# Seven-product pairs from the second pair on in FFN 2 to 4, all weight sums on GpSimd, rows scaled per pair, bank runs in down pairs

## What is computed

```python
for l in range(DEPTH):                       # DEPTH = 2
    x = x + 0.5 * swiglu(rmsnorm(x, norm_w[l, 0]), ffn_w_gate[l, 0], ffn_w_up[l, 0], ffn_w_down[l, 0])
    h = rmsnorm(x, norm_w[l, 1])
    ...                                      # y = mLSTM mixer (l = 0) or gated linear attention (l = 1)
    x = x + y
    x = x + 0.5 * swiglu(rmsnorm(x, norm_w[l, 2]), ffn_w_gate[l, 1], ffn_w_up[l, 1], ffn_w_down[l, 1])
out = rmsnorm(x, final_norm_w)

def rmsnorm(x, w):
    xf = x.astype(jnp.float32)
    y = xf * lax.rsqrt(jnp.mean(xf * xf, axis=-1, keepdims=True) + EPS)
    return (y * w.astype(jnp.float32)).astype(x.dtype)

def swiglu(x, w_gate, w_up, w_down):
    return (jax.nn.silu(x @ w_gate) * (x @ w_up)) @ w_down
```

## Time and profile before

| | |
|---|---|
| median of 3 runs | 2209.91 us (2209.09 to 2210.4) |
| the profiled execution | 2210.02 us, its span 2208.2 us |
| granted TensorE clock, mean | 0.994 |
| PE busy | 2171.4 us, 98% of the span, 16360 matmuls |
| DVE, ACT, POOL busy | 1436.5, 937.9, 236.1 us |
| chain that ended last | PE 93%, DVE 4%, ACT 2% |

### The profile page before, as it was taken

How to read it: one execution, slowest core, us unless ns; L and a number is a source line. 1 busy time by engine, 2 the same in 40 slices (tenths; PEclk the granted TensorE clock), 3 DMA queues, 4 the chain that set the end, 5 groups by cost and what they waited for, 6 DMA issues and landing times.

```text
span 2208.2 us, 40072 instructions
## 1 busy us (share of the span) xinstructions
PE 2171.4 (98%) x16360; PEld 2148.8 (97%) x16360; DVE 1436.5 (65%) x2031; ACT 937.9 (42%) x1371; POOL 236.1 (11%) x186
## 2 busy tenths in 40 slices
PE   7999999999999999999999999999999999999997
PEld 7999999999999999999999999999999899999997
DVE  6797546585555787636678863754766457876365
ACT  5435435454433444525444452544322434445252
POOL 0112010001100002101000210100011101021110
PEclk9999999999999999999999999999999999999998
DMA  5223312223332222222322222232122222223222
GB/s 186 70 87 102 106 67 86 95 83 136 101 118 81 81 93 86 91 82 87 108 72 87 86 95 96 88 94 88 47 98 84 97 77 87 87 88 104 85 77 72
DMA packets 72574, 201.55 MB, mean 91 GB/s; under 512 B 7268, under 2 KB 26980, under 8 KB 72448
## 3 DMA queue, kind: packets, MB, share of 16 engines
q1 hardware_dynamic: 72448, 199.80, 27.7%
HBM read 187.82 MB, written 11.95 MB: 90 GB/s over the span
## 4 chain that ended last, share of the span: by engine, by line
PE 93%; DVE 4%; ACT 2%; issue 1%; DMA 0%; POOL 0%; SPq 0%; DVEq 0%; POOLq 0%
PE ps L525 49%; PE ps L583 33%; PE ps L800 4%; PE ps L655 1%; PE ps L831 1%; PE ps L820 1%; DVE w_lo L1821 1%; PE ps L834 0%; PE ps L850 0%; PE ps L664 0%; DMA x<-in_x 0%; PE ps L678 0%; PE ps L843 0%; PE ps L844 0%; DVE x L2641 0%
## 5 line engine op out<-in xcount | busy, mean ns | idle before, releaser
L525 PE MATMUL ps<-h_lo,w_hi 128*128 128x288 f32 x1616 | 351.4, 297 | 4.1 <-DVE h_hi L2306 4.1
L525 PE MATMUL ps<-h_hi,w_hi 128*128 128x288 f32 x1616 | 351.1, 296 | 0.7 <-DVE w_lo L1821 0.7
L583 PE MATMUL ps<-th_hi,w_hi 128*128 128x288 f32 x1088 | 320.9, 295 | 0.7 <-DVE ps L1916 0.7
L583 PE MATMUL ps<-th_hi,w_lo 128*128 128x288 f32 x1088 | 321.2, 295 | 0.0
L583 PE MATMUL ps<-th_lo,w_hi 128*128 128x288 f32 x1088 | 320.4, 294 | 0.0
L525 PE MATMUL ps<-h_hi,w_lo 128*128 128x288 f32 x1360 | 295.1, 296 | 0.0
L1821 DVE TENSOR_TENSOR w_lo<-raw,w_hi 128x1024 fp32r<-128x1024 f32 x196 | 232.0, 1220 | 65.7 <-ACT w_hi L1232 64.0
L525 PE MATMUL ps<-xn_hi,w_hi 128*128 128x288 f32 x1152 | 257.4, 301 | 11.7 <-DVE w_lo L1821 9.5
L525 PEld LDWEIGHTS ps<-h_lo,w_hi 128*128 128x128 f32 x1616 | 262.6, 189 | 4.8 <-DVE h_hi L2306 4.5
L525 PEld LDWEIGHTS ps<-h_hi,w_hi 128*128 128x128 f32 x1616 | 262.6, 189 | 1.0 <-DVE w_lo L1821 0.9
L525 PE MATMUL ps<-xn_lo,w_hi 128*128 128x288 f32 x1152 | 252.1, 296 | 0.0
(11 more groups left out here) (292 smaller groups left out, 4226.8 us busy)
## 6 DMA issues: line engine op xcount, KB each, us to landing
raw<-in_w_gu SPq DMA_DIRECT2D x176, 512.0 KB, 3.9
raw<-in_w_down SPq DMA_DIRECT2D x64, 512.0 KB, 4.3
raw<-in_w_mix SPq DMA_DIRECT2D x64, 512.0 KB, 4.2
raw<-in_w_down SPq DMA_DIRECT2D x32, 384.0 KB, 3.6
state_s<-in_state_c SPq DMA_DIRECT2D x4, 1024.0 KB, 7.8
out_c_s<-state_s SPq DMA_DIRECT2D x4, 1024.0 KB, 4.6
state_s<-in_state_g SPq DMA_DIRECT2D x4, 1024.0 KB, 6.6
out_s_s<-state_s SPq DMA_DIRECT2D x4, 1024.0 KB, 4.7
```

The lines of the kernel that those rows point to most:

```text
L525: ins = nc.tensor.matmul(o, a, b[:, c] if c is not None else b, start=first and j == 0, stop=last and j == 2)
L583: ins = nc.tensor.matmul(ps[:, bank, FIRST], left, b_, start=first and k == 0 and j == 0, stop=k == KT_X // 2 - 1 and j == 2, skip_group_c ...
```

## The change

In FFN 2 to 4 the plain pairs of group 0 fall from 5 to 1 (`PLAIN`); FFN 1 keeps 5. For this the tile sums of these FFNs are made in the phase ahead, on the last D or OUT phase: `x_ready` adds `early_even`, `u_sums`, `u_high` and `u_low` to the work per down pair. All four weight sums are GpSimd's (`pair_sums`), and in group 0 they wait until the squares have been added (`ssq_done`). `weights_low` now waits for the fourth. x is no longer scaled (`t_sums`, `t_high` are gone); every seven-product pair is scaled by `rows_scale`. The sums over the partitions are fed into PE's second block of pair 0 (`feed_sums`), ACT reads them with Ln and makes `rstd` with Exp, and PE waits after pair 0 for the Ln (`var_ready`), in FFN 1 too. In down pairs of `half` 0 the second block is done in bank runs. Signs of sums change.

```diff
-SEVEN_FROM = 5
+PLAIN = (5, 1, 1, 1)
...
                         if first_norm and half == 0:
-                            ins = token_sums(ph["norm"])
-                        ins.then_inc(pe_done, 1)
-                if consumer:
+                            pe.wait_ge(var_ready, ph["norm"] + 1)
+                if consumer and ph["skip"] > 1:
                     iteration(0, first_norm=True, bank_wait=ph["base"] > 0, by_bank=(1,))
                     iteration(1)
                     iteration(2, seven=(1,))
                     iteration(3, seven=(0, 1))
+                elif consumer:
+                    iteration(0, first_norm=True, seven=(1,))
+                    with pe.Fori(1, ph["pairs"] // 2) as i:
+                        iteration(i, seven=(0, 1))
                 else:
                     with pe.Fori(0, ph["pairs"] // 2) as i:
-                        iteration(i, seven=(0, 1) if ph["kind"] == "G" else ())
+                        iteration(i, by_bank=(0,) if ph["kind"] == "D" else (),
+                                  seven=(0, 1) if ph["kind"] == "G" else ())
...
+            def feed_sums(norm):
...
+                pe.wait_ge(ssq_done, 4 * (norm + 1))
...
+                for c in range(2):
+                    ins = nc.tensor.matmul(ps[:, 5 + 2 * c, FIRST], ones, half_of(T(5), c), start=True, stop=True)
+                ins.then_inc(feed_done, 1)
...
+            def feed_log(ph):
+
+                act.wait_ge(feed_done, ph["ffn"] + 1)
+                nc.scalar.activation(cut2(T(7)), ps[:, 5:8:2, FIRST], ACT.Ln, bias=eps[:, :], scale=1.0 / D_MODEL)\
+                    .then_inc(var_ready, 1)
+
+            def feed_root(n):
+
+                act.wait_ge(var_ready, n + 1)
+                nc.scalar.activation(rstd[:, :], T(7), ACT.Exp, scale=-0.5).then_inc(rstd_ready, 1)
...
+            def x_ready(j, ph, pp):
+
+                norm = ph["norm"] + 1
+                if pp and feeds(j):
+                    u_high(PHASES[j + 1], pp - 1)
+                act.wait_ge(psum_free, ph["base"] + pp + 1)
+                if norm < N_NORMS - 1:
+                    xn_high(norm, 2 * pp)
+                    xn_high(norm, 2 * pp + 1)
+                squares(norm, pp)
+                if feeds(j):
+                    early_even(PHASES[j + 1], pp)
...
+                pool.wait_ge(raw_full[2 * half], 8 * (pair - half) + 16)
+                pool.wait_ge(raw_full[2 * half + 1], 8 * (pair - half) + 16)
+                total(1, raw_unit(half, S3_AT), raw_unit(half, W11_AT), raw_unit(half, S1_AT), ALU.subtract)
+                total(2, raw_unit(half, S1_AT), raw_unit(half, S1_AT), raw_unit(half, W22_AT), ALU.add)
+                total(3, s2(half), raw_unit(half, S1_AT), raw_unit(half, W11_AT), ALU.subtract)
+                if w > 1:
+                    pool.wait_ge(unit_lo, 4 * (w - 1))
+                if ph["group"] == 0 and half == 0:
+                    pool.wait_ge(rstd_ready, ph["norm"] + 1)
+                total(4, s4(half), raw_unit(half, W12_AT), s2(half), ALU.subtract)
...
+                    if ph["group"] == 0:
+                        pool.wait_ge(ssq_done, 4 * (ph["norm"] + 1))
...
                 dve.wait_ge(hi_done, 2 * (ph["base"] + 2 * i + half) + 1)
+                dve.wait_ge(sums_full[half], sums_at(ph, i, half) + 4)
...
-                if before and ph["group"] == 0:
+                if before:
                     rows_scale(ph, *before)
-                if not last:
-                    sum_2(ph, *after)
-                if before:
                     rows_product(ph, *before)
-                if not last:
-                    sum_4(ph, *after)
...
+            def x_ready(j, ph, pp):
+
+                norm = ph["norm"] + 1
+                if norm < N_NORMS - 1:
+                    xn_low(norm, 2 * pp)
+                    xn_low(norm, 2 * pp + 1)
+                add_squares(norm, pp)
+                if feeds(j):
+                    if pp:
+                        u_low(PHASES[j + 1], pp - 1)
+                    u_sums(PHASES[j + 1], pp)
...
+                elif ph["skip"] == 1:
+                    u_low(ph, 3)
+                    sums_early(ph, 0, 1)
+                    dve.wait_ge(pe_done, ph["base"] + 1)
+                    dve.wait_ge(rstd_ready, ph["norm"] + 1)
+                    evac_g(ph, 0, 0)
```

More of the change, by code:

```diff
@@ L48, in schedule @@
             for g, (k0, k) in enumerate(GROUPS):
[L49 removed]
+                skip = 0 if g else PLAIN[ffn]
                 skipped = [(skip + 1 - half) // 2 for half in range(2)]
                 out.append(dict(kind="G", pairs=k, base=pair, ffn=ffn, norm=norm, k=KT_X, k0=k0,
[L52 to L53 removed]
+                                group=g, hidden=hidden, seven=seven - skip, plain=sum(PLAIN[:ffn]), skip=skip,
                                 by_half=[by_half[half] - skipped[half] for half in range(2)]))
@@ L301, in sums_at @@
         def sums_at(ph, i, half):
[L303 removed]
+            return 4 * (ph["by_half"][half] + i)
         def step(i, half):
@@ L500, in _ @@
                     continue
[L501 to L506, removed]
+                with sp.Fori(1 if j == 0 else 0, ph["pairs"] // 2) as i:
                     for half in range(2):
@@ L1291, in seven_rest @@
                     split(PHASES[j + 1], 0, 0)
+                else:
+                    sums_high(ph, *step(i, half))
             def seven_rows(ph, i, half, last):
                 m = 2 * i + half
-                w, pair, b = ph["seven"] + m, ph["base"] + m, 4 * half
-                if ph["group"]:
-                    act.wait_ge(pe_done, pair + 1)
-                    nc.scalar.activation(cut2(T(0)), ps[:, b:b + 2, FIRST], ACT.Silu).then_inc(gate_done, 1)
-                else:
-                    act.wait_ge(gate_ready, ph["scaled"] + m + 1)
-                    nc.scalar.activation(T(0), T(0), ACT.Silu).then_inc(gate_done, 1)
+                w, pair = ph["seven"] + m, ph["base"] + m
+                act.wait_ge(gate_ready, w + 1)
+                nc.scalar.activation(T(0), T(0), ACT.Silu).then_inc(gate_done, 1)
                 if not last:
@@ L1368, in g_phase @@
                         seven_half(i, 1)
+                elif ph["skip"] == 1:
+                    u_high(ph, 3)
+                    weights_high(ph, 0, 1)
+                    sums_high(ph, 0, 1)
+                    feed_log(ph)
+                    feed_root(ph["norm"])
+                    evac_g(ph, 0, 0, lambda: seven_start(ph, 0, 1))
+                    seven_half(0, 1)
+                    with act.Fori(1, n - 1) as i:
+                        seven_half(i, 0)
+                        seven_half(i, 1)
                 else:
```

191 lines of the change are left out of this document (70 added, 121 removed).

## The result

The change makes the kernel slower. Four runs of it have a median of 2242.3 us (2238.92 to 2244.82), against 2209.5 us before (2208.4 to 2210.4); the ratio is 1.0148, with a 95% interval of 1.013 to 1.0165. The direction was forecast, the size was not: I said 2218 us, with a range up to 2237. The profiled execution has a span of 2238.4 us, 30.2 more than before.

What follows compares the result with a forecast made beforehand. PE bounds the kernel, busy for 98% of the span, so time is matmuls times pace plus stops. Terms -17.6 - 10.5 + 20.3 + 1.4 + 4.9 + 10 = +8.5 us on 2209.9 gave 2218 us; range 2196 to 2237.

Steps and rivals of the forecast that it cites:

- Twelve pairs: Group 0 of FFN 2 to 4: four plain pairs each become seven-product pairs, 44.4 us for 50.3, three times: -17.6 us.
- FFN 1: Start of FFN 1: PE waits after pair 0 for the Ln, while an earlier idle and its clock loss go: +1.4 us.
- last groups: Last down phases: two row scalings delay the last pair's rows, +0.9 us in three FFNs, 2.2 in the very last: +4.9.
- DVE operations that are queued without a wait between them I let run through: Starts and seven-product pairs: GpSimd sums get in only where a DVE operation waits for the one before, 1.29 us each.
- the starts: Start of FFN 2 to 4: PE stands for late `weights_low` and Ln, with slower clock and FFN 3's down phase: +20.3 us.
- The slow clock: Behind each longer PE stop at the start of FFN 2 to 4, the granted clock falls, costing 1.6 us each.
- the other pairs: Later seven-product pairs: GpSimd's turns delay DVE; half of about 48 pairs stop by 0.4 us: +10 us, bounds 0 and +24.
- 1.4 us that I had counted as free: Later seven-product pairs: the part sum ends at 1281.4, the W22 product comes at 1282.8, leaving 1.4 us of slack.
- If a run does the same in a down phase, all plain matmuls after the first block go at 130.0: Down phases: a bank run sets the pace from 133.3 to 130.0 ns: -0.9 us in 8 phases, -0.7 in 3.
- the last ones and QK: Last groups' down phases gain 0.7 us each in three; half of each mixer's 400 plain QK matmuls counted: -1.2 us.
- the bank runs: Down phases and QK parts: the faster pace after bank runs brings -10.5 us together, bounds 0 and -12.
- the rival of a turn every time: A waiting GpSimd sum gets in at every turn, also between queued operations: starts +24, pairs +24, 2236 us; chance 0.07.

Runs made afterwards that it cites:

- hold_back: Changed kernel, but in group 0 of FFN 2 to 4 GpSimd's sums for the second seven-product pair wait for `weights_low` of the first; 2238.2 us, ratio 1.013.
- sums_split: Changed kernel with the third and fourth weight sums of every seven-product pair back on DVE, GpSimd keeping two; 2225.4 us, ratio 1.0068 to the kernel before.
- runs_one: Kernel before the change, plus one bank run in each down phase (first pair alone) instead of the change's two; 2202.6 us, ratio 0.9959.
- plain5: Changed kernel with five plain pairs in group 0 of all four FFNs, as before the change; 2227.4 us, ratio 1.008 to the kernel before.

## Why the prediction was wrong

**Twelve pairs, FFN 1, last groups.** These held: the `Ln` wait came to 1.5 us (1.4 said, though its terms 4.2 - 1.9 - 0.7 make 1.6), the rows of the last pairs to 0.82 us in each of three FFNs (0.9) and 3.05 in the very last phase (2.2).

**The step that failed: "DVE operations that are queued without a wait between them I let run through".** It stood on one row, a GpSimd product with 1024 columns, and was applied to the weight sums. I went through all rows of the changed kernel in which a weight sum begins while a DVE operation with both inputs in SBUF runs and another such one follows at once: 91 places. In 13 the follower waited for the one before it, in 78 it was queued (its row begins before the other ends). In 87 of the 91 the sum went in between. In the other four, all queued, the sum's row begins 0.03 to 0.08 us after that of the follower, and DVE went first. So in all 91 the one whose row begins first goes first, queued or not. In the kernel before, eight weight sums met a follower that waited, GpSimd first each time, and none came ahead of a queued one. What did come ahead of queued operations and yet ran behind them were two 1024-column products, that of the earlier trace rows and this one:

```profile
1643.89 0.74 DVE L2471 TENSOR_TENSOR qt<-qt,raw 128x576 f32<-128x576 f32 x1
1644.03 3.62 POOL L1796 TENSOR_TENSOR k_tok_b<-k_hl,cst 128x1024 fp32r<-128x1024 f32 x1
1644.55 1.34 DVE L2306 TENSOR_TENSOR h_hi<-scratch,h_lo 128x1152 fp32r<-128x1152 f32 x1
```

So the trace of before held nothing on what a weight sum does to queued operations. I had bridged that with a row of another operation, and gave the case in which a sum gets in at every turn 7 in 100.

The Trainium skill (SBUF — State Buffer, "Who interferes with whom") has the shared ports as an exclusive lock, and says that the order of issue decides who blocks. The 91 places agree with it, if the beginning of a row is taken for the issue; the two 1024-column products do not, and no run here says why.

This step fed two terms. At the starts, the third step of `u_sums` (L1972) is queued behind the second, and a sum gets in: `u_sums` ends at T + 13.2 (12.4 said), and with it the Ln comes at T + 18.4 (17.6 said). `u_low` then meets a sum that began 0.09 us before it, a turn that I had not counted, while the one ahead of `weights_low` I had. Together `weights_low` ended at T + 19.1 (17.2 said), and the idle was 5.5 to 6.2 us (4.0 to 5.0 said). `hold_back` took the turns ahead of `u_low` and `weights_low` away and left the later Ln: 4.8 us in FFN 2 and 4. The slow clock cost 4.9 us (4.8 said), which is luck in part: 1.2, 1.3 and 2.4 us where I had 1.6 each. In the other pairs +10 became +20.8, and `sums_split` took 12 of the 14.9 us in groups 1 and 2 back. A pair of group 1 of FFN 3, DVE and POOL:

```profile
1283.15 1.79 POOL L1799 TENSOR_TENSOR scratch<-raw 128x512 f32<-128x512 f32 x1
1284.05 1.45 DVE L1889 TENSOR_TENSOR w_lo<-raw,w_hi 128x512 fp32r<-128x512 f32 x1 [0.26 <-ACT w_hi L1259]
1285.02 1.62 POOL L1799 TENSOR_TENSOR scratch<-raw,scratch 128x512 f32<-128x512 f32 x1
1285.41 1.84 DVE L1927 TENSOR_TENSOR h_lo<-scratch,h_hi 128x576 f32 x1
...
1288.92 0.45 DVE L1947 TENSOR_TENSOR ps<-ps,scratch 128x288 f32<-128x288 f32 x1
```

A low part of weights takes 1.45 for 0.68 and that of the rows 1.84 for 0.75. With two scalings more ahead of them, the part sum of 1288.92 is done at 1289.37, and PE starts the W22 product at 1289.43. Of 1.4 us that I had counted as free nothing is left. Leaving out the first one of each FFN 2 to 4, 50 of 77 seven-product pairs take over 0.1 us more than their 11.11, 0.43 us on average. I had said 24 pairs and 0.4 us: the size of a stop was right, their number was not.

**The second step that failed: "If a run does the same in a down phase, all plain matmuls after the first block go at 130.0".** In a full down phase a run does not set the pace, it switches it. The second run of each phase gave back what the first had gained, so that the eight phases brought 4.4 us and the last ones and QK nothing. `runs_one` brought 1.0 us a phase by leaving the second out.

**The sizes.** Of the 20.6 us between the account and the prediction, 10.8 are the other pairs, 6.1 the bank runs, 3.0 the starts and 0.7 the rest. With the rival of a turn every time (2236 us) and the bank runs at their measured value (+6.1) the sum would have been 2242 us. That this is the measured median is luck in part: the two terms of that rival are 48 us, and measured they are 44.1.

**Open.** What makes the pace: why a run of 48 matmuls always switches it and one of 36 seldom, and what set it in the OUT phase of the first mixer, where no run stands. And why the 1024-column product of GpSimd lets queued DVE operations pass.

## What to carry to other kernels

Before work is given to an idle GpSimd, find DVE's operations with two inputs in SBUF that stand on the chain: each can be held for a whole GpSimd operation, in queued rows too, whatever the busy shares say. For a rule about who goes first, count all the places in the trace instead of resting on one, and look at whose row begins first. When a pattern seems to change an engine's pace, look at what the next repetition of it does before multiplying by the number of phases.

## What was not expected of the hardware

- Two paces of the same plain matmuls with alternating banks, 133.3 and 130.0 ns: each run of 24 + 24 matmuls in one bank each switched from one to the other and back (all eight full down phases, two runs in each). Runs of 18 + 18 switched nothing in the changed kernel, but did at two places of `hold_back` and one of `plain5`.
- Between a weight sum of GpSimd and a queued DVE operation, both with two inputs in SBUF, hundredths of a us decide: the one whose row begins first goes first, and the other stands until it is done (91 of 91 places in the changed kernel).
- The granted clock falls for a time that is not the same from place to place. An idle of 0.77 us in the first mixer cost nothing in the kernel before, but in `runs_one` the window around it shows 0.67, with 55 matmuls instead of 79:

```profile
470.00:480.00 10.00, 9.23 (x55) 0.67 0.51 167
```

It may be part of why executions of one kernel differ by some us; that was not tried. The start of FFN 4 had two such windows where FFN 2 had one, with the same idle:

```profile
720.00:730.00 10.00, 5.66 (x32) 0.83 0.17 54
...
1830.00:1840.00 10.00, 4.46 (x28) 0.84 0.07 21
1840.00:1850.00 10.00, 10.00 (x65) 0.82 0.38 129
```
